# A decoder trunk on one core: products of zeros during TensorE's waits, left out

## The reference

```
for layer in range(2):
    mix = even_mixer(x, ...) if layer == 0 else odd_mixer(x, ...)
    x = layer_norm(A * x + mix, ...)                                    # norms 0, 3
    x = layer_norm(A * x + memory_cross_attention(x, mem_k, mem_v), ...) # norms 1, 4
    x = layer_norm(A * x + hierarchical_moe(x, ...), ...)               # norms 2, 5
```

## The kernel before, in words

| place | products | the wait behind it |
|---|---|---|
| input projection, layer 0 | 8 | first weights loaded |
| norms 0, 1, 3, 4, half t = 1 | 10 each | `n_ready` |
| norm 2, halves t = 0 and t = 1 | 20 and 10 | `n_ready` |
| input projection, layer 1 | 8 | `xT` of norm 2 |
| queries, layers 0 and 1 | 6 each | `xT` of norms 0 and 3 |
| places, layers 0 and 1 | 15 each | mask ready |
| first gather, layers 0 and 1 | 6 each | banks 4 to 6 drained |

## Time and profile before

### The profile page before, as it was taken

The page is one execution under the profiler, slowest core; times in us unless marked ns, Lnnn a source line. Parts: engine busy times, 40 slices in busy tenths (PEclk is TensorE's granted clock), DMA queues, the critical chain, the costliest instruction groups (busy, mean ns, idle before and its releaser), DMA issues.

```text
span 1691.8 us, 19144 instructions
## 1 busy us (share of the span) xinstructions
PE 1624.4 (96%) x6961; PEld 940.5 (56%) x6971; DVE 357.1 (21%) x755; ACT 166.7 (10%) x401; POOL 61.8 (4%) x84
## 2 busy tenths in 40 slices
PE   7999999999999999999999999998999999999995
PEld 6874566545544644554458756554464455456441
DVE  1963432511100100110042132410011011001103
ACT  0212301000000000000010001000000000000000
POOL 3000010100000000000010010100000000000001
PEclk9999999999999999999999999899999999999998
DMA  9565021479989989998982352306899899899981
GB/s 329 185 205 193 0 102 73 174 283 390 392 356 394 392 373 377 393 394 354 389 301 86 136 207 94 124 0 256 354 393 385 363 395 392 357 393 394 384 364 58
DMA packets 63186, 473.12 MB, mean 280 GB/s; under 512 B 4092, under 2 KB 9532, under 8 KB 38572
## 3 DMA queue, kind: packets, MB, share of 16 engines
q1 hardware_dynamic: 60940, 465.78, 68.4%
q0 software_dynamic: 2208, 6.81, 1.3%
HBM read 471.52 MB, written 1.05 MB: 279 GB/s over the span
## 4 chain that ended last, share of the span: by engine, by line
PE 92%; DVE 4%; issue 1%; DMA 1%; another core or an unknown queue 1%; ACT 1%; DVEq 0%; POOL 0%; ACTq 0%; SPq 0%; POOLq 0%
PE bank L827 27%; PE bank L817 15%; PE bank L845 13%; PE bank L460 12%; PE bank L853 7%; PE bank L473 7%; PE bank L636 2%; PE bank L834 1%; DMA ring<-in_ev_w_in_dram 1%; DVE x L960 1%; PE bank L591 1%; PE bank L435 1%; PE bank L762 1%; DVE xT L969 1%
## 5 line engine op out<-in xcount | busy, mean ns | idle before, releaser
L827 PE MATMUL bank<-ring,kT 128*64 128x512 f32 x2048 | 446.4, 593 | 2.5 <-DVE kT L1269 2.0
L827 PEld LDWEIGHTS bank<-ring,kT 128*64 128x64 f32 x2048 | 170.5, 137 | 275.4 <-issue 275.2
L817 PEld LDWEIGHTS bank<-prob,x 128*128 128x128 f32 x1024 | 246.9, 335 | 25.0 <-issue 24.3
L817 PE MATMUL bank<-prob,x 128*128 128x128 f32 x1024 | 253.0, 405 | 0.0
L845 PE MATMUL bank<-ring,probT 128*64 128x512 f32 x1056 | 234.8, 597 | 0.2 <-ACT probT L1520 0.2
L460 PE MATMUL bank<-xT,ring 128*128 128x256 f32 x832 | 183.3, 382 | 6.8 <-DMA ring<-in_ev_w_in_dram 3.4
L460 PEld LDWEIGHTS bank<-xT,ring 128*128 128x128 f32 x832 | 158.5, 191 | 31.3 <-issue 5.9
L1273 DVE SCALAR_TENSOR_TENSOR probT<-probT,bank 128x512 f32<-128x512 f32 x33 | 22.7, 687 | 672.9 <-ACT probT L1516 672.9
L845 PEld LDWEIGHTS bank<-ring,probT 128*64 128x64 f32 x1056 | 73.2, 137 | 157.4 <-issue 156.8
L853 PE MATMUL bank<-prob 128*128 128x512 f32 x256 | 118.6, 607 | 0.0
L473 PE MATMUL bank<-ring,oT 128*128 128x512 f32 x256 | 110.8, 593 | 3.8 <-issue 1.9
(11 more groups left out here) (275 smaller groups left out, 879.1 us busy)
## 6 DMA issues: line engine op xcount, KB each, us to landing
ring<-in_moe_w_dram SPq DMA_DIRECT2D x192, 2048.0 KB, 12.3
ring<-in_od_w_in_dram SPq DMA_DIRECT2D x6, 2048.0 KB, 15.9
ring<-in_ev_w_in_dram SPq DMA_DIRECT2D x4, 2048.0 KB, 16.3
ring<-in_xa_wq_dram SPq DMA_DIRECT2D x4, 2048.0 KB, 12.9
ring<-in_xa_wo_dram SPq DMA_DIRECT2D x4, 2048.0 KB, 11.1
ring<-in_mem_wk_dram SPq DMA_DIRECT2D x2, 2048.0 KB, 14.8
ring<-in_mem_wv_dram SPq DMA_DIRECT2D x2, 2048.0 KB, 12.2
ring<-in_ev_w_out_dram SPq DMA_DIRECT2D x2, 2048.0 KB, 7.9
```

Source lines behind the costliest of these rows:

```text
L817: ins = mm(bY[k // 4][:, (k % 4) * P:(k % 4 + 1) * P], src, d[:, t, :, :].rearrange("p e s -> p (e s)"), start=(t == 0), stop=(t == TT - 1))
L827: ins = mm((b1, b3)[m][j * CAP:(j + 1) * CAP, :], xg[:, k, j * CAP:(j + 1) * CAP], w[:, k, :], start=(k == 0), stop=(k == KC - 1))
```

## The change

`keep_warm` and its seven call sites go. The products that it issued are not issued; nothing else is moved or added, no wait is taken away, and no other engine's list changes.

```diff
-            def keep_warm(ps, n):
-                for _ in range(n):
-                    mm(ps[:, :], zero16[:, 0:P], zero16[:, :], start=True, stop=True)
...
                         ps = claim(pe, (key, t, h))
                         if key[0] == "n" and h == 0:
-                            if t == 1 or key[1] % 3 == 2:
-                                keep_warm(ps, (20, 10)[t])
                             pe.wait_ge(n_ready, 2 * key[1] + t + 1)
...
                 if c == 0:
-                    keep_warm(ps, 8)
                     wait_loaded(pe, "av")
...
                             if h == 0 and c == 0:
-                                keep_warm(ps, 8)
                                 wait_xT(("n", 2))
...
                     if j == 0:
-                        keep_warm(ps, 6)
                         wait_xT(("n", 3 * L))
...
                 ps = claim(pe, ("pos", L))
-                keep_warm(ps, 15)
                 pe.wait_ge(mask_ready, L + 1)
...
                 pe.wait_ge(bank_drained[7], fills[7])
-                keep_warm(banks[7], 6)
                 for b in range(4, 7):
                     pe.wait_ge(bank_drained[b], fills[b])
```

## The result

| | before | after |
|---|---|---|
| median of 11 runs each | 1695.44 us | 1707.5 us |
| profiled execution, first to last instruction | 1691.8 us | 1706.4 us |
| mean granted clock of it | 0.987 | 0.970 |
| PE busy | 1624.4 us | 1612.9 us |

The ratio of after to before is 1.0072, 95% interval 1.0054 to 1.0091: slower by 0.72%, about 12 us. (One of the runs after took 6011 us without any stretch at half clock; the ratio leaves it out.) TensorE is busy for less time and the kernel takes longer.

What follows compares the result with a forecast made beforehand. TensorE, busy 1624.4 of 1691.8 us, was taken as the bound. Place terms 0.4 + 2.4 + 4.4 + 1.7 + 2.4 - 1.9 = +9.4 us gave 1701.2 us, plus 7.3 us 1708.5 us; range 1702.0 to 1714.0 us.

Steps and rivals of the forecast that it cites:

- nowhere new: Rival, whole kernel: clock falls at no new place, only delays in norms 2 and 4 go; -2.8 us, 1696.3 us; chance 0.05.
- only in the expert stages: Rival: transposes hold the clock before the query projections, so norms 0 and 3 cost nothing; +4.6 us, 1703.7 us; chance 0.12.
- half clock for long: Rival: clock stays at half through the gathers into the hidden products; +5 us over the forecast, about 1714 us; chance 0.10.
- start: First weights and projection: rest grows from 3.4 to 6.2 us, half clock may begin earlier or last longer; +0.4 us.
- norm 0 and queries: Transposes at half clock 0.4 us, query projection starting at half 2.0 us; +2.4 us, from +1.0 to +3.6.
- norm 1, router, gather: Transposes 0.4 us, router at half 3.07 us, place products 0.9 us, gather neglected; +4.4 us, from +3.1 to +5.3.
- norm 2 and projection: Late products gone, -0.3 us; layer 1's projection starts at half clock, 2.0 us; +1.7 us, from -0.6 to +3.
- norm 3 and queries: Same as norm 0: transposes at half clock and query projection starting at half; +2.4 us.
- norm 4, router, gather: Router already at half; late products go -3.1 us, place products +0.9, transposes +0.3; -1.9 us, from -3.1 to -0.8.
- one of four such places lost the clock: Norms 0, 1, 3, 4: 2.2 us rest behind ten zero products is at the edge; one loss in four taken as average.
- about 0.8 us: Transposes in the norms: what would leave the sum if, by the Trainium skill's rule, they cost the same at either clock.
- The 7.3 us between span and median: Added to the 1701.2 us span for what lies around it and executions losing the clock elsewhere; gives 1708.5 us.

Runs made afterwards that it cites:

- e4: Against the kernel before, only norm 2's 20 and 10 zero products and the 8 ahead of layer 1's input projection left out; ratio 1.0016, 2.7 us.
- e2: Against the kernel before, only the 10 zero products ahead of the second half of norms 1 and 4 left out; ratio 1.0028, 4.7 us.
- e6: Against the kernel before, 19 zero products instead of 10 ahead of the second half of norms 0, 1, 3 and 4; ratio 1.0029.
- e12: Against the kernel before, 18 one-column zero products (36 real instructions) added behind the 8 at the start; ratio 1.0020, 3.4 us.
- e10: Against the kernel before, 19 zero products instead of 10 in norms 0, 1, 3 and 4, others left out to keep the list's length; ratio 0.9976.
- e8: Against the kernel before, all zero products left out but for 19 ahead of the second half of norms 1 and 4; ratio 1.0029, 4.9 us.
- e7: Against the kernel before, 19 zero products in norms 0, 1, 3, 4; 18 at the start, 16 in norm 2's first half, 12 before layer 1's projection; ratio 1.0042.
- e3: Against the kernel before, only the 15 zero products ahead of the place products and the 6 ahead of the first gather left out, both layers; ratio 1.0007.
- e9: Against the kernel before, 36 empty instructions added behind the 8 zero products at the start, which never reached the list; ratio 0.9996.
- e11: Against the kernel before, 19 zero products in norms 0, 1, 3, 4 with list length kept, and 16 and 14 in norm 2; ratio 0.9984.

## Why the prediction was right

**Direction and mechanism.** What the zero products had done for the clock went with them, and only the late ones (ahead of norm 2's transposes and behind a slowed router) gave time back. Each step that named a rest and a half clock behind it shows in the profile after. The rivals "nowhere new" and "only in the expert stages" fall with the query projections at 0.82 and 0.91; "half clock for long" falls too, although the clock did stay at half for 20.5 and 23.9 us around the two routers, because the gather does not feel it. The halving that the Trainium skill states (TensorE: Matmul & The Clock Gate, "Part 1: The HAM clock gate") fits the dense projections (6.0 us at half cost 3.1 us behind norm 0) and not the gather, as the prediction's rows had it.

**Sizes, by place over all profiles.** The 14 profiles hold each place several times, with the products that before has there and without any. (Kernels that have another number of products at a place are not counted there.) The table gives the number of profiles and their mean time, lowest and highest in brackets, from a fixed instruction ahead of the place to one behind it. At the start that is from the first instruction to the end of the 64th product. In norms 0 and 3 it is from the second half normalized to the end of the 64th query product. In norm 2 it is from the first half normalized to the end of the 64th product of layer 1's projection. In norms 1 and 4 it is from the second half normalized to the first product of the first expert pair.

| place | with: profiles, us | without: profiles, us | difference | forecast |
|---|---|---|---|---|
| start | 9: 30.5 (29.6 to 31.8) | 3: 32.4 (32.2 to 32.5) | +1.9 | +0.4 |
| norm 0 and queries | 7: 17.0 (17.0 to 17.0) | 3: 19.7 (19.2 to 20.7) | +2.8 | +2.4 |
| norm 1, router, gather | 6: 23.9 (20.6 to 26.4) | 1: 25.3 | +1.4 | +4.4 |
| norm 2 and projection | 9: 21.9 (21.8 to 22.2) | 3: 24.0 (23.5 to 24.4) | +2.1 | +1.7 |
| norm 3 and queries | 7: 17.3 (17.0 to 18.0) | 3: 19.7 (19.1 to 20.7) | +2.4 | +2.4 |
| norm 4, router, gather | 6: 26.1 (25.0 to 26.7) | 1: 25.3 | -0.8 | -1.9 |

The differences make 9.8 us, the forecast's sum was +9.4 us, and the timed ratio says about 12 us (9 to 15). The sum is right partly by luck. The change costs its time at the start and in the dense projections (9.2 us), and hardly at the routers (0.6 us for both, forecast 2.5 us), since before had mostly lost those already and paid for late products besides. The start was put 1.5 us too low and the routers 1.9 us too high.

**The step that was wrong.** The prediction took the profile of before as an average one: four equal rests of 2.2 us behind ten products, "one of four such places lost the clock". Over the seven profiles that have before's products at a place the places are not alike. Norms 0 and 3, with six more products ahead of their projection, kept the full clock up to the 64th product in 12 of 14 cases; behind norms 1 and 4 the router was slowed in 12 of 14, and in the ten of these that had the 15 products the place products began 1.0 to 3.2 us after the mask was ready. Why the same rest behind the same ten products ends so differently no run settles. The profile of before had one of the only two routers at full clock, that of norm 1, and so the prediction charged the change 4.4 us there. The change's own profile confirmed it with 4.8 us, but only because the comparison is with the same lucky profile.

**Smaller terms.** The projections behind norms 0, 2 and 3 cost 3.1, 2.1 and 1.4 us beyond 13.9 us, not 2.0 us each: the mean, 2.2 us, was near, the spread wider than the single row of the start suggested. The second half's transposes ran wholly at half each time and took 1.94 us, +0.8 us where the forecast had 0.4; the prediction's "about 1.8 us" for them would by its own figures have been 1.96 us (0.88 us at half for 0.52 us at full). Its "about 0.8 us" for all transpose terms is a slip as well: with 0.4 us in norms 0, 1 and 3 and 0.3 us in norm 4 they make 1.5 us. In norm 2 the 0.3 us to be gained did not come in the changed kernel: the first half's transposes took 1.9 us at half for 1.16 us, and GpSimd started later behind its data. With the clock still full there, in e4, the gain was 0.5 us; that working was sound.

The attention's 3.2 us and the 1.2 us gained in the second round belong to alignment, not to the change: profiles without any edit near the attention show the same fall at 150 us or not (11 of the 14 profiles have it between 149 and 153 us, for 3.4 or 6.8 us; those of before, e2 and e4 do not).

**The reference.** The 7.3 us between span and median were not mostly what lies around the span: each execution's own time stands about 1.8 us above its span (1708.17 us against 1706.4 us for the profiled one after). The profiled execution of before, about 1693.6 us by this, was a little faster than the middle one, and the median of more runs came down from 1699.06 to 1695.44 us. That 1707.5 us lies 1.0 us from the forecast owes something to chance: a level taken 3.6 us too high, and an effect taken 3 us too small.

**Runs of one kernel.** The clock also orders the runs in which nothing differs. Of 113 runs of the kernel before, timed beside the experiments, the 31 with the lowest mean clock (0.982 to 0.984) took 1700.2 us on average, and the 12 with the highest (0.991 and more) 1688.2 us. No edit is behind this, so by itself it shows that the two go together, not which leads.

**Single removals.** They add up: 1.0021, 1.0028, 1.0007, 1.0016 and 1.0000 make +0.72%, the change's own ratio, though each has an interval of about 0.2% to either side and four of the five touch none. What is shown for each by the clock in its profile is firmer than its time.

## What to carry to other kernels

Work that nobody reads can be worth its place: ahead of a wait it may hold TensorE's clock for what stands behind the wait, and the price of leaving it out is read off the real products after the rest, not off its own busy time. One profile of a kernel whose clock sits at an edge is one draw: count the place over several profiles before calling it the normal case. And when instructions are added, look at the waits under "issue" in the whole trace, since a longer list can cost as much far behind the edit as the edit brings; keep the list's length equal when the effect of something else is to be measured.

## What the runs showed of the hardware that was not expected

- Instructions added early in a list brought a stall 850 us later: with 36 more, TensorE stood idle for 5.3 us behind the first expert loop with nothing to wait for, whether they were 18 wide products in the norms (e6) or 18 products of one column at the start (e12). With 110 fewer ahead of it (after), or as many (e10), it did not. It is not length beyond a limit either: e8, with a shorter list than before, had a stall of 2.6 us behind the second loop, and e7 one of 3.5 us near the beginning of the first. Why the length decides was not tried further.
- Two levels of clock make no difference to the gather of 128-column products (7.88 us at a mean clock of 0.70 in e3 and of 0.76 and 0.62 in after, 7.88 us at 1.00 in before), while the same clock costs the router of 36-column products 3.07 us of 3.81 us.
- The 36 empty instructions of e9, with nothing to wait for or to signal, did not reach TensorE's list.
- With ten zero products ahead of a rest of 2.2 us, norms 0 and 3 and the projection behind them (six more products between) kept the full clock in 12 of 14 cases, the routers behind norms 1 and 4 in 2 of 14.
- With 10 zero products ahead of the second half, 2 of 14 routers ran in 3.81 us; with 19, 7 of 10 (kernels e6, e7, e8, e10, e11) ran in at most 3.81 us, and the other three in 4.14 to 4.42 us.
